# Stick q and k, gates and projections of the gated sum made with weight tiles as left operands

## The reference

```python
h = _rms(x, g_norm1) * (1 + sc1) + sh1
proj = h @ w_in
c_q, c_kv, k_pe, q_sb, k_sb, v_sb, gl_a, gl_b = split(proj)   # 512, 512, 64, 3 x 1024, 2 x 2048
y_a = mla_attention(...)                 # 8 heads, from the latents c_q and c_kv
y_b = stick_breaking(q_sb, k_sb, v_sb)   # 8 heads of 128

# stick breaking, scale = 128 ** -0.5, mask: key before query
z = (q @ k.T) * scale
log_one_minus = where(mask, log_sigmoid(-z), 0)
tail = reverse_cumsum(log_one_minus) - log_one_minus
a = where(mask, exp(log_sigmoid(z) + tail), 0)
y_b = a @ v

merged = sigmoid(gl_a) * (y_a @ w_proj_mla) + sigmoid(gl_b) * (y_b @ w_proj_sb)
x = x + gt1 * (merged @ w_out)
# then the feed-forward part of the block
```

## The kernel before

| chunks G | product | chunks |
|---|---|---|
| 0 to 15 | latents c_q and c_kv | 16 |
| 16 | key product: k_pe, 64 features (`pe_key_product`, L2321) | 1 |
| 17 to 24 | first 512 features of stick q | 8 |
| 25 to 38 | from the latents to MLA's q, k, v | 14 |
| 39 to 78 | rest of stick q (8), k (16), v (16); from 44 on also MLA's heads | 40 |
| 79 to 142 | gates gl_a and gl_b; stick groups beside them, 16 chunks apart | 64 |
| 143 to 174 | projections y_a @ w_proj_mla and y_b @ w_proj_sb, 4 chunks each in turn | 32 |
| 175 to 206 | merged @ w_out | 32 |

## Time and profile before

### The profile page before, as it was taken

How to read it: one execution, slowest core, us unless ns; L and a number is a source line. 1 busy time by engine, 2 the same in 40 slices (tenths; PEclk the granted TensorE clock), 3 DMA queues, 4 the chain that set the end, 5 groups by cost and what they waited for, 6 DMA issues and landing times.

```text
span 2606.9 us, 33516 instructions
## 1 busy us (share of the span) xinstructions
PE 2587.1 (99%) x11881; PEld 2145.5 (82%) x11881; DVE 1825.4 (70%) x2168; ACT 1414.8 (54%) x1861; POOL 14.6 (1%) x28
## 2 busy tenths in 40 slices
PE   9999999999999999999999999999999999999999
PEld 7888888878888888888788888888788888888887
DVE  5888888777777878888875545566687654445565
ACT  6555545465656465445566556544465556565443
POOL 1000000000000000000000000000000000000000
PEclk9999999999999999999999999999999999999999
DMA  7765556778888888887665555555578765655554
GB/s 247 253 194 178 170 151 205 268 262 291 283 292 285 291 285 297 283 293 253 199 202 157 167 171 160 184 204 186 183 269 289 254 198 191 195 190 197 192 193 172
DMA packets 302590, 582.20 MB, mean 223 GB/s; under 512 B 20133, under 2 KB 20913, under 8 KB 302097
## 3 DMA queue, kind: packets, MB, share of 16 engines
q1 hardware_dynamic: 301008, 576.26, 66.7%
q0 software_dynamic: 1008, 3.55, 0.4%
q10 hardware_dynamic: 464, 0.93, 0.1%
HBM read 578.55 MB, written 2.11 MB: 223 GB/s over the span
## 4 chain that ended last, share of the span: by engine, by line
PE 95%; DVE 3%; ACT 1%; issue 1%; DMA 0%; ACTq 0%; DVEq 0%
PE acc L328 30%; PE acc L330 30%; PE acc L329 30%; DVE lo L315 1%; PE aux L1131 1%; DVE op_lo L509 0%; PE tp L482 0%; DVE op_hi L508 0%; ACT stage L494 0%; PE tp L1105 0%; PE aux L2258 0%; PE aux L2257 0%; PE tp L542 0%; DMA rows<-attn_norm_w 0%; PE tp L1151 0%
## 5 line engine op out<-in xcount | busy, mean ns | idle before, releaser
L315 DVE TENSOR_TENSOR lo<-raw,hi 128x1024 fp32r<-128x1024 f32 x895 | 1077.2, 1222 | 430.5 <-ACT hi L309 409.6
L309 ACT ACTIVATE hi<-raw 128x1024 fp32r<-128x1024 f32 x895 | 928.3, 1056 | 528.5 <-PE acc L330 368.8
L328 PE MATMUL acc<-hi,op_hi 128*128 128x512 f32 x2752 | 1084.9, 394 | 8.5 <-DVE lo L315 5.9
L330 PE MATMUL acc<-hi,op_lo 128*128 128x512 f32 x2752 | 1072.1, 390 | 0.0
L329 PE MATMUL acc<-lo,op_hi 128*128 128x512 f32 x2752 | 1071.5, 389 | 0.0
L328 PEld LDWEIGHTS acc<-hi,op_hi 128*128 128x128 f32 x2752 | 516.9, 188 | 119.6 <-issue 11.2
L330 PEld LDWEIGHTS acc<-hi,op_lo 128*128 128x128 f32 x2752 | 516.6, 188 | 109.0
L329 PEld LDWEIGHTS acc<-lo,op_hi 128*128 128x128 f32 x2752 | 517.2, 188 | 102.6
L591 DVE SCALAR_TENSOR_TENSOR ada_acc<-ada_ring,cact,ada_acc 128x512 f32<-128x512 f32 x360 | 269.5, 749 | 7.6 <-DVE small L431 0.6
L328 PE MATMUL acc<-hi,f_hi 128*128 128x512 f32 x704 | 274.5, 390 | 0.1
L329 PE MATMUL acc<-lo,f_hi 128*128 128x512 f32 x704 | 273.9, 389 | 0.0
(11 more groups left out here) (336 smaller groups left out, 1284.0 us busy)
## 6 DMA issues: line engine op xcount, KB each, us to landing
raw<-w_in SPq DMA_DIRECT2D x257, 512.0 KB, 3.9
ada_ring<-w_ada SPq DMA_DIRECT2D x192, 512.0 KB, 5.3
raw<-w_gate_up SPq DMA_DIRECT2D x176, 512.0 KB, 5.2
raw<-w_ffn_in SPq DMA_DIRECT2D x176, 512.0 KB, 4.4
raw<-w_down SPq DMA_DIRECT2D x88, 512.0 KB, 5.8
raw<-w_ffn_out SPq DMA_DIRECT2D x88, 512.0 KB, 4.3
raw<-w_out SPq DMA_DIRECT2D x64, 512.0 KB, 4.1
raw<-w_proj_mla SPq DMA_DIRECT2D x16, 512.0 KB, 3.9
```

The costliest lines, as they stand in the source:

```text
L309: A.activation(hi[:, k, :, 0:n], raw[:, k, :, 0:n], ACT.Copy).then_inc(hi_ready, 1)
L315: V.tensor_tensor(lo[:, k, :, 0:n], raw[:, k, :, 0:n], hi[:, k, :, 0:n].bitcast(F32), ALU.subtract).then_inc(lo_ready, 1)
L328: T.matmul(dst, lh, hi[:, k, kk, 0:n], start=first and kk == 0, stop=False)
L330: mm = T.matmul(dst, ll, hi[:, k, kk, 0:n], start=False, stop=last and kk == CK - 1)
```

## The change

The feature side and the token side of four products change places. In `pe_turned` the left operand is a 128x128 tile of weights (hi or lo) and the right operand is all 256 tokens of the activations. A chunk's 512 output features become four tiles of 128; each gets 256 columns of the bank pair, and a chunk is 2 x 4 x 3 = 24 matmuls of 256 columns. The result has features on the partitions, and nothing has to be turned later.

It is used for stick q (chunks 17 to 24 and the first 8 from 39 on), stick k (the next 16), the gates (64) and the projections (32). Stick v and the rest keep `pe_chunk`. The stick groups read q and k (`turned_head`) and v directly from `proj`; the scale is put into q's readout; slots 2, 3 and 6 of a group and the tiles `s_in` and `s_qk` are gone. The first score product waits for the readouts of banks 14 and 15 (those of v, which follow the ones of k), and the wait for `tp` moves to slot 8. ACT waits for the last stick output ahead of the last gate's readout, which writes over part of v. `pe_merged` is gone: ACT makes `op_hi` straight from the gated sum (`act_merged`) and DVE `op_lo`.

```diff
@@ -330,6 +328,20 @@
                     mm = T.matmul(dst, ll, hi[:, k, kk, 0:n], start=False, stop=last and kk == CK - 1)
                 if t == 0 and half is not None:
                     mm.then_inc(half, 1)
+            mm.then_inc(chunk_used, 1)
+
+        def pe_turned(pe, c, into, kt, first, last, right=(op_hi, op_lo)):
+
+            k = c % RING
+            pe.wait_ge(lo_ready, c + 1)
+            for kk in range(CK):
+                rh, rl = (o[:, kt + kk] for o in right)
+                for f in range(NB // P):
+                    dst = into[:, f // 2, f % 2 * S:(f % 2 + 1) * S]
+                    wh, wl = (r[:, k, kk, f * P:(f + 1) * P] for r in (hi, lo))
+                    T.matmul(dst, wh, rh, start=first and kk == 0 and f % 2 == 0, stop=False)
+                    T.matmul(dst, wh, rl, start=False, stop=False)
+                    mm = T.matmul(dst, wl, rh, start=False, stop=last and kk == CK - 1 and f % 2 == 1)
             mm.then_inc(chunk_used, 1)
 
         def pe_acc_wait(pe, b, i, per):
...
@@ -1743,6 +1755,13 @@
             c0 = j * NB if j < 7 else FREE0 - ROPE
             return proj[:, :, c0:c0 + NB]
 
+        def turned_head(which, head):
+            c0 = SB0 + which * DH + head // 4 * NB + head % 2 * S
+            return proj[:, head % 4 // 2, c0:c0 + S]
+
+        def merged_pair(g):
+            return gate_cols(g // 2)[:, g % 2]
+
         def in2_src(G):
             if G < 2 * 8:
                 b, k = G // 8, G % 8
...
 
-        def act_read2(act, n, dst, func):
+        def act_read2(act, n, dst, func, scale=1.0):
             done2(act, n)
-            A.activation(dst, acc[:, bank2(n)], func).then_inc(acc_free[bank2(n)], 1)
+            A.activation(dst, acc[:, bank2(n)], func, scale=scale).then_inc(acc_free[bank2(n)], 1)
+
+        def act_merged(act, g):
+            act.wait_ge(gated, g // 2 + 1)
+            if g >= 4:
+                act.wait_ge(chunk_used, C2 + G_OUT - 7 + g)
+            A.activation(op_hi[:, CK * g:CK * g + CK].rearrange("p k s -> p (k s)"), merged_pair(g), ACT.Copy).then_inc(merged_hi, 1)
 
         def act_latent_squares(act, l):
             act.wait_ge(acc_free[bank2(l)], freed2(l))
@@ -1916,18 +1941,6 @@
                 A.activation(m_pt[:], tp[:, :, 0:TRI], ACT.Copy).then_inc(ml["pt"], 1)
 
         def act_stick(act, g, at):
-            if at == 2:
-                if g == 0:
-                    act.wait_ge(ml["o"], GROUPS)
-                    act.wait_ge(acc_free[bank2(15)], freed2(15))
-                else:
-                    act.wait_ge(sk["o"], g)
-                src = proj[:, :, SB0:FREE0].rearrange("p t (d n) -> p t d n", d=3)[:, :, :, g * GW:(g + 1) * GW]
-                for t in range(TT):
-                    A.activation(s_in[:, t], src[:, t], ACT.Copy).then_inc(sk["in"], 1)
-            if at == 6:
-                act.wait_ge(sk["tr"], g + 1)
-                A.activation(s_qk[:, :, 0:S], tp[:, :, 0:S], ACT.Copy, scale=float(P) ** -0.5).then_inc(sk["q"], 1)
             if at == 8:
                 act.wait_ge(sk["z"], g + 1)
                 A.activation(s_l[:], aux[:, :, 0:TRI], ACT.Abs).then_inc(sk["l"], 1)
...
                     elif n < 11:
                         if n == 4:
                             act.wait_ge(lt["split"], LG)
                         act_read2(act, n, proj[:, :, (n - 4) * NB:(n - 3) * NB], ACT.Copy)
                     elif n < 16:
-                        act_read2(act, n, proj[:, :, SB0 + (n - 10) * NB:SB0 + (n - 9) * NB], ACT.Copy)
+                        act_read2(act, n, proj[:, :, SB0 + (n - 10) * NB:SB0 + (n - 9) * NB], ACT.Copy,
+                                  float(P) ** -0.5 if n == 11 else 1.0)
                     elif n < 24:
+                        if n == 23:
+                            act.wait_ge(sk["o"], GROUPS)
                         act_read2(act, n, gate_cols(n - 16), ACT.Sigmoid)
                 if G == 14:
                     act_angles(act)
...
@@ -2111,7 +2124,11 @@
                 V.tensor_tensor(s_b[:], s_b[:], heads_of(sbmask), ALU.mult).then_inc(sk["a"], 1)
 
         def dve_second(dve, cd, out_readout):
-            merged = lambda g: dve_operand(dve, cd, OG["merged"], 8, 0, only=[g])
+            def merged(g):
+                dve.wait_ge(merged_hi, g + 1)
+                h, l = (o[:, CK * g:CK * g + CK].rearrange("p k s -> p (k s)") for o in (op_hi, op_lo))
+                V.tensor_tensor(l, merged_pair(g), h.bitcast(F32), ALU.subtract).then_inc(merged_ready, 1)
+
             after = dve_second_steps(dve, "in2", xw2)
             for G in range(G_END):
                 if G == 0:
...
                 ins.then_inc(ml["o"], 1)
 
         def pe_stick(pe, g, at):
-            if at == 3:
-                pe.wait_ge(sk["in"], g * 2 + 2)
-                if g:
-                    pe.wait_ge(sk["w"], g)
-                else:
-                    pe.wait_ge(ml["pt"], GROUPS)
-                for h in range(GH_HEADS):
-                    for j in range(2):
-                        for t in range(TT):
-                            ins = T.transpose(tp[:, h, (2 * j + t) * P:(2 * j + t + 1) * P], s_in[:, t, j, h * P:(h + 1) * P], ident)
-                ins.then_inc(sk["tr"], 1)
             if at == 5:
-                pe.wait_ge(sk["q"], g + 1)
-                pe.wait_ge(sk["k"], g + 1)
+                if g == 0:
+                    for n in (14, 15):
+                        pe.wait_ge(acc_free[bank2(n)], freed2(n))
                 if g:
                     pe.wait_ge(sk["op"], g)
                 else:
                     pe.wait_ge(ml["op"], GROUPS)
                 for h in range(GH_HEADS):
-                    q, kk = s_qk[:, h, 0:S], s_qk[:, h, S:2 * S]
+                    q, kk = (turned_head(j, GH_HEADS * g + h) for j in range(2))
                     T.matmul(aux[:, h, 0:S], kk[:, 0:P], q, start=True, stop=True)
                     ins = T.matmul(aux[:, h, S:TRI], kk[:, P:S], q[:, P:S], start=True, stop=True)
                 ins.then_inc(sk["z"], 1)
             if at == 8:
                 pe.wait_ge(sk["n"], g + 1)
+                if g:
+                    pe.wait_ge(sk["w"], g)
+                else:
+                    pe.wait_ge(ml["pt"], GROUPS)
                 for h in range(GH_HEADS):
                     causal_product(tp[:, h], (after, ones), s_n[:, h])
                     ins = T.matmul(tp[:, h, S:TRI], after, s_n[:, h, S:TRI], start=True, stop=True)
@@ -2304,19 +2315,9 @@
             if at == 11:
                 pe.wait_ge(sk["a"], g + 1)
                 for h in range(GH_HEADS):
-                    ins = causal_product(aux[:, h], [s_in[:, t, 2, h * P:(h + 1) * P] for t in range(TT)], s_b[:, h])
+                    c0 = SB0 + 2 * DH + (GH_HEADS * g + h) * P
+                    ins = causal_product(aux[:, h], [proj[:, t, c0:c0 + P] for t in range(TT)], s_b[:, h])
                 ins.then_inc(sk["o"], 1)
-
-        def pe_merged(pe, g):
-            j = g // 2
-            pe.wait_ge(gated, j + 1)
-            Gm = OG["merged"] + g
-            pe.wait_ge(stage_ready, CK * (Gm - 1))
-            for kk in range(CK):
-                for t in range(TT):
-                    col = (CK * (g % 2) + kk) * P
-                    ins = T.transpose(tp[:, Gm % 2, kk * S + t * P:kk * S + (t + 1) * P], gate_cols(j)[:, t, col:col + P], ident)
-            ins.then_inc(tp_ready, 1)
 
         def pe_key_product(pe, c, b):
             pe.wait_ge(lo_ready, c + 1)
@@ -2338,8 +2339,10 @@
                     h2(G)
                 if G == 16:
                     pe_key_product(pe, c, B2 + n)
+                elif 16 < G < G_UP:
+                    pe_turned(pe, c, into, CK * (G - 17), G == 17, G == G_UP - 1)
                 elif G < G_UP:
-                    k = G % 8 if G < 16 else G - 17
+                    k = G % 8
                     pe_chunk(pe, c, 0, 4, into, CK * k, k == 0, k == 7, late=OG["h2"] + 1 if G == 0 else None)
                 elif G < G_SB:
                     k = (G - G_UP) % 2
@@ -2348,19 +2351,22 @@
                     pe_chunk(pe, c, 0, 4, into, kt, k == 0, k == 1, left=(lat_hi, lat_lo))
                 elif G < G_PP:
                     k = (G - (G_SB if G < G_GATE else G_GATE)) % 8
-                    pe_chunk(pe, c, 0, 4, into, CK * k, k == 0, k == 7)
+                    if G_SB + 24 <= G < G_GATE:
+                        pe_chunk(pe, c, 0, 4, into, CK * k, k == 0, k == 7)
+                    else:
+                        pe_turned(pe, c, into, CK * k, k == 0, k == 7)
                 elif G < G_OUT:
                     k = (G - G_PP) % 4
                     if (G - G_PP) % 8 < 4:
                         pe.wait_ge(ml["op"], GROUPS)
-                        pe_chunk(pe, c, 0, 4, into, CK * (k % 2), k == 0, k == 3, left=(ya_hi[k // 2], ya_lo[k // 2]))
+                        pe_turned(pe, c, into, CK * (k % 2), k == 0, k == 3, right=(ya_hi[k // 2], ya_lo[k // 2]))
```

(34 more changed lines are left out.)

## The result

| | before | after | ratio of the two |
|---|---|---|---|
| median | 2608.8 us | 2620.55 us (2620.35 to 2621.21) | 1.0046, 95% interval 1.0031 to 1.006 |
| span of the profiled execution | 2606.9 us | 2618.9 us | |

The change costs 11.8 us (8 to 16 by the interval). The forecast was 7.4 us less, with a range up to 2610 us. The result lies 1.7 us from rival 2, which had 2622.2 us.

What follows compares the result with a forecast made beforehand. PE was taken to bound the kernel. Removed transposes gave -7.4 us, turned chunks, ACT and DVE work and new waits 0: span 2606.9 to 2599.5, plus 1.8 around it, 2601.3 us; range 2599.5 to 2610.

Steps and rivals of the forecast that it cites:

- rival 2: Turned matmuls: loads cause the excess, a 128-wide one beside 256 columns costs 13.5 ns, pitch 120.2, 2622.2 us; chance 0.13.
- What bounds the kernel: PE is busy for 99% of the span, so time is a sum of matmul times, with almost no stall to win.
- Part 1, the removed transposes: Four groups of 8 (stick q and k) and eight groups of 4 (gated sum) go: -7.4 us together.
- Part 2, the turned chunks: 128 chunks become 24 matmuls of 256 columns instead of 12 of 512, at 113.4 ns each: cost 0.
- the two limits: Turned matmul's pitch: 113.4 ns from the key product (256 columns, 64-wide weights), 111.4 from plain fp32 matmuls with full loads.
- The rule cited against the change: Weight loads overlap matmuls only across different row groups, never with full 128x128 tiles; each turned matmul would carry its load bare.
- Rival 1: Turned matmuls: the full load's hand-over adds 2.6 ns to 113.4, pitch 116.0, bill 8.0 us, 2609.3 us; chance 0.20.
- Rival 4: A wait appears or PE's queue runs short; half-chunk stalls in four stick groups, 5.4 us, 2606.7 us; chance 0.04.
- The cushion for the gated sum: Time from the gated sum's operand being complete to PE needing it in the last product: from 5 to over 8 us.
- ACT and DVE: Stick copies, the q and k eviction and some gated-sum split work go from engines that end nothing: worth 0.

Runs made afterwards that it cites:

- the shapes: Kernel before, its eight gate products' split matmuls given other weight and moving columns, work left out; ran once, 2628.17 us, only pitches compared (128/256: 119.9 ns).
- the gain alone: Kernel after with its 128 turned chunks back to 12 matmuls of 512 columns, the 64 transposes still away, values wrong: 2601.14 us, ratio 0.9971.
- the half: Kernel after with only stick q and k turned (32 chunks), gates and projections as before, values right: 2609.2 us, ratio 1.0001.

## Why the prediction was wrong

- **What bounds the kernel: right.** PE for the whole of the stretch, no waits, before and after.
- **Part 1, the removed transposes: right.** -7.4 us forecast, -7.4 measured alone. Reading each group's time from the chain of waits was enough.
- **Part 2, the turned chunks: the step that failed.** "I take the larger of the two limits, 113.4 ns (nearest in type and columns), so part 2 costs 0." Both readings stand again in the experiments: 111.7 ns for full loads with few columns, 113.3 for 256 columns beside a 64-wide load. The step that failed is taking 113.4, measured beside a half-wide load, as the limit that 256 columns set beside a full one. Beside full loads the columns need 13.3 ns over a column per cycle and not 6.7, at 256 columns as at 512, so the pitch is 119.9 ns. That the two limits lie close to each other is not shown to be the reason: at 320 columns, far above the load's 111.7 ns, full fp32r loads still take 146.7 against 140.0 in bf16. The term is +18.9 us instead of 0 (20.0 by the pitch, 1.1 less as shown), and of the 19.2 us between forecast and result that is all but 0.3.
- **The rival that came out, by half of its reason.** Rival 2's 120.2 ns and 2622.2 us are right to 0.3 ns and 1.7 us. It carried the 13.5 ns of excess beside full loads from 512 to 256 columns, and the table bears that out. Its reason, that loads cause all of the excess over a column per cycle, in proportion to their width, is not borne out: full bf16 loads leave most of the excess (225.0 at 512), narrow loads at 512 columns cost more and not less, and 32 and 64 wide take the same 113.3 at 256. What is shown is smaller: at 256 columns a full fp32r load costs 6.6 ns that a 64-wide, a 32-wide or a bf16 one does not, and a 96-wide one costs 2.8.
- **The evidence that I set against rival 2** was one start: the 512-column matmul ahead of the key product took 0.23 us with a 64-wide load beside it. It was a true observation, but of 512 columns, where a narrower load doesn't help; it said nothing of 256. It was also a single step, read to 0.01 us, to tell 0.23 from the rival's 0.22. It should not have taken the rival's chance down to 0.13.
- **The rule cited against the change** (the Trainium skill, "TensorE: Matmul & The Clock Gate", "What overlaps and what doesn't") pointed the right way, but not for its reason. If a load of some 108 ns (the estimate of the prediction) lay bare on top of 113.3, the pitch would be 221; it is 119.9, so the load overlaps nearly whole, and the price is 6.6 ns. The load rows of the shapes grow by 26 to 31 ns for every 32 columns of fp32r (108, 134, 161 and 188 to 192 ns for 32, 64, 96 and 128). The same page of the Trainium skill, under "LDWEIGHTS (loading the stationary operand)", gives a load of P columns P / 1.2 ns, 26.7 for 32, and there the trace agrees.
- **Rival 1, the hand-over on top, 2.6 ns:** too small; 6.5 were paid over 113.4. **Rival 4, new waits:** none came. The cushion for the gated sum grew, from 8.9 us before (complete at 1793.40, needed at 1802.29) to 12.3 us, in the kernel after (1801.64, 1813.95) as in the gain alone. The prediction had 5 and over 8, because it took the seventh chunk for the eighth and left out the two groups of transposes that lie between.
- **ACT and DVE:** their busy time fell by 8 and 6 us on the page, and it bought nothing, as said.

What stays open: why matmuls with full fp32r loads need 12 to 16 ns over the pure columns from 240 columns on, and lighter loads at 256 columns only half of that. No run here looked at what the two share. Nor is it known why 32- and 64-wide loads beside 512 columns are slower than full ones, or where the 4 to 12 ns over the pure columns come from that bf16 shows too. In `pe_turned` two of three matmuls in a row use the same weights and load them twice; whether one load would do was not tried.

The two versions with right values that were run, the whole change and the half, are not faster than the kernel before. Turning pays where what it saves is over 0.16 us a chunk (24 x 119.9 ns less 12 x 226.8). Stick q and k save 3.6 us in 32 chunks, 0.11 a chunk; gates and projections 3.8 us in 96, 0.04. The table has no cheaper cut for the turned product either: 240 columns take 112.9 ns, but 256 tokens don't divide by it, and two matmuls of 128 take 2 x 111.8.

## What to carry to other kernels

When an edit doubles the number of matmuls at the same number of columns, take the pitch for exactly that pair of load width and columns from a run or a trace. A row with the right columns and a narrower load is no substitute: here it gave 113.3 ns, and the full load took 119.9. The trace of before held a better neighbour, the 13.5 ns by which the 512-column matmuls with full loads exceed a column per cycle. With thousands of instances a few ns decide, so where the trace lacks the pair, the range has to reach both neighbours. Separate gain and loss into two kernels, one that leaves out what the edit removes and one that adds what it adds; here -7.4 and +18.9 us explained the +11.8 at once.

## What the runs showed of the hardware that I had not expected

- With full fp32r weights, one load for every matmul, the pitch is flat at 111.7 ns up to 224 columns and rises with the columns from 240 on: 112.9 at 240, 119.9 at 256, 226.8 at 512. So between 240 and 224 columns lies the point where cutting a matmul shorter stops paying.
- Narrower weights can be slower: beside 512 columns 230.0 ns for 64 and 231.6 for 32 columns of weights, against 226.8 for 128. At 384 columns all are within 2 ns (173.3 to 175.0).
- A full bf16 load lasts 96 ns against 188 to 192 for fp32r, and in bf16 (every second element read) 128 columns go in 57.3 ns instead of 111.8; at 512 columns bf16 wins only 1.8 ns a matmul.
- After small products the 512-column matmuls run long for a few turns, 23 ns in all behind each group; the 256-column ones don't. That gave back 1.1 us.
